# A chunked linear recurrence: its triangular inverses in 32x32 diagonal blocks on 32x32 array tiles, in a new order

## What is computed

```python
def step(S, inp):
    r_t, w_t, k_t, v_t, kk_t, a_t = inp
    sa = jnp.einsum("bhvk,bhk->bhv", S, -kk_t)
    S = (S * w_t[:, :, None, :] + sa[..., None] * (kk_t * a_t)[:, :, None, :]
         + v_t[..., None] * k_t[:, :, None, :])
    o_t = jnp.einsum("bhvk,bhk->bhv", S, r_t)
    return S, o_t
```

## Time and profile before

| | |
|---|---|
| median of three runs | 2034.57 us |
| the profiled execution | 2037.52 us, of which the span is 2035.8 us |
| mean granted TensorE clock | 0.979 |
| PE / PEld busy | 93% / 80% |
| DVE / ACT / POOL busy | 50% / 40% / 12% |
| DMA | 505.55 MB, mean 248 GB/s |
| recurrence, from the span's start | about 526 to 880 us |

### The profile page before, as it was taken

How to read it: one execution, slowest core, us unless ns; L and a number is a source line. 1 busy time by engine, 2 the same in 40 slices (tenths; PEclk the granted TensorE clock), 3 DMA queues, 4 the chain that set the end, 5 groups by cost and what they waited for, 6 DMA issues and landing times.

```text
span 2035.8 us, 49583 instructions
## 1 busy us (share of the span) xinstructions
PE 1890.3 (93%) x20798; PEld 1623.3 (80%) x20798; DVE 1014.0 (50%) x1676; ACT 814.9 (40%) x1436; POOL 244.5 (12%) x308
## 2 busy tenths in 40 slices
PE   7999999999999999999999999999999899777797
PEld 6988999999888888879998676776777677343597
DVE  6644463544455555624544643434445444577344
ACT  4234232334555555523333333333333444555233
POOL 0200000000243444413200000000000000010032
PEclk8999999999999999989999999999999999899899
DMA  7535455544133322105488999999999999999541
GB/s 283 172 135 172 167 172 171 169 162 162 55 100 91 91 88 85 53 22 191 151 328 318 419 419 416 405 425 425 425 424 426 399 420 380 416 366 374 237 145 73
DMA packets 122383, 505.55 MB, mean 248 GB/s; under 512 B 15969, under 2 KB 55266, under 8 KB 76898
## 3 DMA queue, kind: packets, MB, share of 16 engines
q1 hardware_dynamic: 122178, 502.60, 64.6%
HBM read 470.24 MB, written 32.32 MB: 247 GB/s over the span
## 4 chain that ended last, share of the span: by engine, by line
PE 30%; DMA 17%; DVE 2%; issue 2%; SPq 2%; ACT 1%; DVEq 0%; ACTq 0%
DMA at_vraw<-in_cache_v 17%; PE psP L2502 8%; PE psP L2503 7%; PE psP L2504 7%; PE at_psO L2552 5%; PE at_psS L2531 3%; SPq L1915 1%; PE psP L2597 0%; DVE wlo L2264 0%; PE at_psT L2543 0%; DVE at_o_new L2419 0%; SPq L1933 0%; SPq L2000 0%; SPq L1955 0%; ACT whi L2090 0%
## 5 line engine op out<-in xcount | busy, mean ns | idle before, releaser
L2502 PE MATMUL psP<-xhi,whi 128*128 128x320 f32 x1488 | 475.4, 319 | 2.5 <-DVE xlo L2389 1.9
L2504 PE MATMUL psP<-xhi,wlo 128*128 128x320 f32 x1488 | 460.6, 310 | 0.0
L2503 PE MATMUL psP<-xlo,whi 128*128 128x320 f32 x1488 | 460.4, 309 | 0.0
L2502 PEld LDWEIGHTS psP<-xhi,whi 128*128 128x128 f32 x1488 | 280.3, 188 | 65.8 <-issue 65.1
L2264 DVE TENSOR_TENSOR wlo<-wraw,whi 128x2048 fp32r<-128x2048 f32 x92 | 213.0, 2315 | 206.2 <-ACT whi L2090 206.0
L2090 ACT ACTIVATE whi<-wraw 128x2048 fp32r<-128x2048 f32 x92 | 176.0, 1913 | 275.4 <-PE psP L2504 274.1
L2503 PEld LDWEIGHTS psP<-xlo,whi 128*128 128x128 f32 x1488 | 280.6, 189 | 0.1
L2504 PEld LDWEIGHTS psP<-xhi,wlo 128*128 128x128 f32 x1488 | 280.2, 188 | 0.0
L131 PE MATMUL psP<-xhi,whi 128*128 128x320 f32 x704 | 218.1, 310 | 3.0 <-DVE wlo L166 2.3
L132 PE MATMUL psP<-xlo,whi 128*128 128x320 f32 x704 | 217.5, 309 | 0.0
L133 PE MATMUL psP<-xhi,wlo 128*128 128x320 f32 x704 | 217.5, 309 | 0.0
(11 more groups left out here) (359 smaller groups left out, 3255.8 us busy)
## 6 DMA issues: line engine op xcount, KB each, us to landing
wraw<-in_weights SPq DMA_DIRECT2D x160, 1024.0 KB, 6.1
at_kraw<-in_cache_k SPq DMA_DIRECT2D x96, 1024.0 KB, 11.3
at_vraw<-in_cache_v SPq DMA_DIRECT2D x94, 1024.0 KB, 10.8
at_kraw<-in_cache_k SPq DMA_DIRECT2D x64, 512.0 KB, 9.9
at_vraw<-in_cache_v SPq DMA_DIRECT2D x62, 512.0 KB, 10.4
rw_s0t<-in_s0T SPq DMA_DIRECT2D x16, 256.0 KB, 3.1
o_wkv_s<-rw_SN SPq DMA_DIRECT2D x16, 256.0 KB, 2.3
resT<-in_xT SPq DMA_DIRECT2D x4, 640.0 KB, 5.8
```

Of the source, the lines that this page charges most:

```text
L2502: pe.matmul(out, wh, c_.xhi[:, kc, :], start=(kc == 0), stop=False)
L2503: pe.matmul(out, wh, c_.xlo[:, kc, :], start=False, stop=False)
L2504: last = pe.matmul(out, wl, c_.xhi[:, kc, :], start=False, stop=(kc == NM - 1))
```

## The change

1. The inverse is made only for the 32x32 diagonal blocks of A: all of D, Dt, D2, D2t, D4t, W, Y, FI, Yt, E, Et, E2t, Z, XD, XDt are compact, 32 columns a chunk on 128 partitions (four blocks: two for each head). A new product `AA` makes the diagonal blocks of A, masked by VectorE into D (inside blocks of 8) and `F` (the rest).
2. The products D2, W, D4t, Y (five chunks) and E, Z1, E2t, X (four chunks) run by `by_fourths` on 32x32 tiles, four products to a chunk. E2, E4t and Z2 are gone: with four blocks of 8 in 32 tokens, E^4 is zero.
3. The transposed copies Dt, D2t, Yt, Et and X1t come from VectorE's 32x32 transposes, SBUF to SBUF, in place of TensorE products and ScalarE copies.
4. The corner block of X (second half from first half of a head's 64 tokens) is X22 A21 X11, by two products `Ht` and `XB` on 64x64 tiles with A12 (masked on ScalarE) and Ht's right half held at the identity; ScalarE writes X's two halves (`Xa`, `XB`). GpSimd spreads Y of chunk 4 into X (`Y4`).
5. `s4` leaves out the quadrant that D of chunk 4 came from.
6. `ORDER` is written anew for all steps. Masks and two constants more are made on GpSimd.

The diff, cut to its core:

```diff
 ORDER = """
-F.a.sq F.a.ka1 R.t.U0 R.a.Q4 R.a.SA4 R.t.Q4 R.a.O0 P.t.AB R.t.SA0 R.g.Vnx R.v.U0 F.v.cs R.t.U4 P.t.s4 R.t.S0
...
+R.t.U0 R.t.Q4 P.t.AA P.t.AB R.g.Vnx R.a.Q4 F.a.sq R.v.U0 R.t.U4 P.v.D R.t.SA0 F.t.ss P.g.ID R.v.SA0 P.v.Dt R.t.S0
+P.v.F R.v.U4 P.t.D2 R.v.ST0 F.v.ssm R.t.U1 R.t.SA4 R.t.O0 F.a.ln R.v.U1 P.v.FR R.t.SA1 R.a.SA4 P.t.Vn R.a.O0 R.a.SP1
+R.v.SA1 R.g.SAx P.a.D2 R.t.S1 R.t.O4 R.v.ST1 P.v.KK R.t.U2 R.a.O4 R.a.SP2 P.a.Vn R.t.SN P.v.D2t P.a.A12 R.v.U2 F.a.kk0
+F.a.ka1 R.t.SA2 R.v.SNa P.t.W P.t.D4t R.v.SA2 P.v.W R.g.SNb P.a.D4t R.t.S2 P.t.Y R.v.ST2 R.a.SP3 R.t.U3 P.v.Y F.a.rn
+R.t.O2 R.v.U3 P.g.Y4 P.v.Yt R.t.O1 F.g.k2 R.a.O2 R.t.SA3 R.a.O1 P.t.E R.v.SA3 F.v.cs R.t.O3 P.a.E P.t.Kn R.a.O3 F.v.kk
+R.t.mean P.v.Et P.a.Kn F.g.ka F.v.rk F.a.Pi P.t.E2t R.v.cen P.t.Z1 F.g.csm P.a.E2t P.t.s4 R.a.csq P.v.Z1 F.a.Pc P.t.X
+F.g.Kz R.t.var F.a.Pm P.v.X P.v.s3 R.t.S3 F.v.Bz F.g.Rz R.a.lnv P.t.Bn P.v.X1t R.v.ST3 R.a.rstd P.t.Ht F.t.bon R.v.on
+P.a.Ht P.t.XB R.a.ong F.v.bonus P.a.Bn F.v.Az R.g.oy P.a.XB P.a.Xa R.g.y R.a.xh R.v.xl
...
-        D, Dt, D2, D2t, D4t, W = (sb(x, [P, CH, L]) for x in ("D", "Dt", "D2", "D2t", "D4t", "W"))
-        Yt, E, Et = (sb(x, [P, NCH, L]) for x in ("Yt", "E", "Et"))
+        D, Dt, D2, D2t, D4t, W, Y = (sb(x, [P, CH, HL]) for x in ("D", "Dt", "D2", "D2t", "D4t", "W", "Y"))
+        FI, Yt, E, Et, E2t, Z, XD, XDt = (sb(x, [P, NCH, HL]) for x in ("FI", "Yt", "E", "Et", "E2t", "Z", "XD", "XDt"))
+        A12, Ht = sb("A12", [P, NCH, L]), sb("Ht", [P, NCH, L])
...
+                    elif name == "Dt":
+                        Q.v.wait(dve, "D", t)
+                        Q.v.done(dve.transpose(flat(Dt[:]), flat(D[:])), name)
...
+                def by_fourths(out, lhs, rhs, n):
 
                     for c in range(n):
+                        for r in fourths:
+                            last = pe.matmul(out[r, c * HL:c * HL + HL], lhs[r, c], rhs[r, c], start=True, stop=True)
+                    return last
+
+                def corner(out, lhs, rhs):
+
+                    for c in range(NCH):
                         for r in halves:
+                            last = pe.matmul(out[r, c * HL:c * HL + HL], lhs[r, c], rhs[r, c], start=True, stop=True)
                     return last
...
+                    elif name == "AA":
+                        F.v.wait(pe, "Az", t)
+                        F.v.wait(pe, "Bz", t)
+                        for c in range(CH):
+                            for g, rows in enumerate(fourths):
+                                r, cols = halves[g // 2], slice(HL * (g % 2), HL * (g % 2) + HL)
+                                last = pe.matmul(ps[rows, c * HL:c * HL + HL], BZ[j][r, c, cols], ar[r, c, 0, cols],
+                                                 start=True, stop=True)
...
                     elif name == "D2":
-                        Q.a.wait(pe, "Dt", t)
-                        Q.t.done(each(ps, Dt, D, CH), name)
-                    elif name == "D2t":
-                        Q.a.wait(pe, "Dt", t)
-                        Q.t.done(each(ps, D, Dt, CH), name)
+                        Q.v.wait(pe, "Dt", t)
+                        Q.t.done(by_fourths(ps, Dt, D, CH), name)
...
+                    elif name == "Ht":
+                        Q.a.wait(pe, "A12", t)
+                        Q.v.wait(pe, "X1t", t)
+                        Q.t.done(corner(ps, A12, XDt), name)
+                    elif name == "XB":
+                        Q.a.wait(pe, "Ht", t)
+                        Q.v.wait(pe, "X", t)
+                        Q.t.done(corner(ps, Ht, XD), name)
...
                         elif name[0:2] == "SA":
                             if c == 0:
-                                Q.v.wait(pe, "X", t)
+                                Q.a.wait(pe, Q.a.last("Xa", "XB"), t)
```

More of the change, by code:

```diff
@@ L328 @@
 ORDER = """
-F.a.sq F.a.ka1 R.t.U0 R.a.Q4 R.a.SA4 R.t.Q4 R.a.O0 P.t.AB R.t.SA0 R.g.Vnx R.v.U0 F.v.cs R.t.U4 P.t.s4 R.t.S0
[L330 to L337, removed]
+R.t.U0 R.t.Q4 P.t.AA P.t.AB R.g.Vnx R.a.Q4 F.a.sq R.v.U0 R.t.U4 P.v.D R.t.SA0 F.t.ss P.g.ID R.v.SA0 P.v.Dt R.t.S0
[6 more added lines that the diff above has]
+P.a.Ht P.t.XB R.a.ong F.v.bonus P.a.Bn F.v.Az R.g.oy P.a.XB P.a.Xa R.g.y R.a.xh R.v.xl
+""".split()
 AT = {x: k / len(ORDER) for k, x in enumerate(ORDER)}
@@ L396, in products_of_chunk @@
     return pe.matmul(out, wl, c_.xhi[:, kc, :], start=False, stop=(kc == NM - 1))
-READ_BY = {"AB": ("v", "D", "FR", "KK"), "s4": ("v", "D4s", "s3"), "Vn": ("a", "Vn"), "Bn": ("a", "Bn"),
[4 rows of a table removed]
-           "SN": ("v", "SNa"), "mean": ("v", "cen"), "var": ("a", "lnv")}
+READ_BY = {"AB": "v.FR v.KK a.A12", "s4": "v.s3", "AA": "v.D v.F", "Vn": "a.Vn", "Bn": "a.Bn", "Kn": "a.Kn",
+           "D2": "a.D2", "W": "v.W", "D4t": "a.D4t", "Y": "v.Y", "E": "a.E", "Z1": "v.Z1", "E2t": "a.E2t",
+           "X": "v.X", "Ht": "a.Ht", "XB": "a.XB", "Q4": "a.Q4", "U4": "v.U4", "SA4": "a.SA4", "O4": "a.O4",
+           "SN": "v.SNa", "mean": "v.cen", "var": "a.lnv"}
 for _c in range(NCH):
-    READ_BY |= {f"U{_c}": ("v", f"U{_c}"), f"SA{_c}": ("v", f"SA{_c}"), f"S{_c}": ("v", f"ST{_c}"),
-                f"O{_c}": ("a", f"O{_c}")}
+    READ_BY |= {f"U{_c}": f"v.U{_c}", f"SA{_c}": f"v.SA{_c}", f"S{_c}": f"v.ST{_c}", f"O{_c}": f"a.O{_c}"}
 class Banks:
@@ L495, in make_masks @@
     made(pool.tensor_copy(m3[:, 2], m3[:, 0]))
-    made(pool.tensor_copy(mFI[:, 1], mSI[:, 1]))
-    made(pool.tensor_tensor(mFI[:, 0], mSI[:, 0], m8[:], ALU.subtract))
+    made(pool.memset(c_.side[:], 0.0))
+    for g in range(4):
+        rows, cols = slice(HL * g, HL * g + HL), slice(HL * (g % 2), HL * (g % 2) + HL)
+        made(pool.tensor_copy(c_.mD[rows, :], m8[rows, cols]))
+        made(pool.tensor_copy(c_.mF[rows, :], mSI[rows, 0, cols]))
+        made(pool.tensor_copy(c_.I4[rows, :], c_.ident[rows, rows]))
+        made(pool.memset(c_.side[rows, g % 2:g % 2 + 1], 1.0))
+    made(pool.tensor_tensor(c_.mF[:], c_.mF[:], c_.mD[:], ALU.subtract))
     made(pool.memset(keep[:], 1.0))
@@ L1392, in free_p @@
                     if tile >= 0:
-                        eng, *by = READ_BY[x]
-                        for y in by:
-                            (Q.v if eng == "v" else Q.a).wait(pe, y, tile)
+                        for y in READ_BY[x].split():
+                            (Q.v if y[0] == "v" else Q.a).wait(pe, y[2:], tile)
             def free_r(name, t):
@@ L1401, in free_r @@
                     if tile >= 0:
-                        eng, *by = READ_BY[x]
-                        for y in by:
-                            (R.v if eng == "v" else R.a).wait(pe, y, tile)
+                        for y in READ_BY[x].split():
+                            (R.v if y[0] == "v" else R.a).wait(pe, y[2:], tile)
             def over_channels(out, mat, x):
@@ L1508, in products @@
                     elif name == "E2t":
                         Q.a.wait(pe, "E", t)
[L1510 to L1520 removed]
+                        Q.v.wait(pe, "Et", t)
@@ L1521, in products @@
+                        Q.t.done(by_fourths(ps, E, Et, NCH), name)
+                    elif name == "X":
                         Q.a.wait(pe, "E2t", t)
                         Q.v.wait(pe, "Z1", t)
-                        Q.t.done(each(ps, D2t, W, NCH), name)
-                    elif name == "X":
-                        Q.a.wait(pe, "E4t", t)
-                        Q.v.wait(pe, "Z2", t)
-                        Q.t.done(each(ps, D4t, Dt, NCH), name)
+                        Q.t.done(by_fourths(ps, E2t, Z, NCH), name)
+                    elif name == "Ht":
[6 more added lines that the diff above has]
+                        Q.t.done(corner(ps, Ht, XD), name)
```

194 lines of the change are left out of this document (114 added, 80 removed), and 4 rows, old and new, of the table READ_BY.

## The result

The changed kernel is slower: 2111.10 us (median of four runs, 2106.52 to 2116.84) against 2033.41 (four runs), a ratio of 1.0384 [1.0357, 1.041]. The prediction was 1982, faster. The profiled execution spans 2107.1 us at a mean granted clock of 0.954 (before 2035.8 and 0.979). The time is lost in the recurrence, which reaches to about 958 us in place of 880.

The account below looks back on a forecast made before the run. TensorE was taken to bound the recurrence, the U0-to-xl run close beside: 17.1 x 1.12, taken as slots of 19.0 for 22.34 us, saves 50 us plus 2.5 in slot 1; 2037.5 - 52.8 = 1984.7 profiled, median 1982, range 1958 to 2025.

Parts of the forecast that it names:

- E2t: Small-tile TensorE product in a slot, among the 328 records at 8 ns each; shares one tile-size visit with Z1.
- The sum of TensorE's work: TensorE's work in a recurrence slot: 19.98 us before, 17.1 after, with 2.62 for 328 small records, 1.33 for tile-size changes.
- The first rival: Every small record costs 28 to 29 ns whatever its size; TensorE's slot sum 24.0 us, time 2070; 8 in 100.
- The transposes and the narrow VectorE steps: On VectorE in each slot: five transposes 1.51 us, narrowed steps 2.25 where about 3.5 before; VectorE's total 13.3 us.
- the new waits: SA0 waits for XB's copy, about 3 us of cover; D2, E, Z1, Ht wait for transposes queued on VectorE.
- the rate of the 328: TensorE's records on 32x32 and 64x32 tiles in a slot: 8 ns each, 2.62 us together.
- The clock rival: More waits and smaller tiles drop TensorE's clock in every slot, losing 2 to 4 us each; about 2030; 8 in 100.
- The factor of 1.12: Slot length over TensorE's sum, 22.34 against 19.98 us before; kept for the new slot, 17.1 x 1.12 = 19.1 us.
- the run: VectorE's in-order chain from U0 to xl in a slot, the second bound: 16.7 us, or 17 with U0 itself.

Follow-up runs that it names:

- the kernel with the early load: The changed kernel with the load of s0t moved to the head of SyncE's part of a slot; 2067.97 us, ratio 1.0167 against the kernel before.
- the filler: The changed kernel with nine unread 128x128 f32 products added on TensorE ahead of Q4's wait; 2080.00 us, one run.
- the kernel before with the late load: The kernel before with the load of s0t moved behind the wait for y, at the end of SyncE's part of a slot; 2125.58 us, one run.
- half the records: The kernel with the early load, its by_fourths group steps made as half as many records on 64x64 tiles (output not the reference's); 2025.28 us, one run.
- the run's end cut off: The kernel of 2024.03 with xh and xl done one slot later and the order planned anew; 1994.74 us, ratio 0.9809 against the kernel before.
- the kernel of 2024.03: The change's algebra in full squares on 64x64 tiles, s0t loaded early, order planned anew; 2024.03 us, ratio 0.9948 against the kernel before.
- the fourth stretch of the small products: Last of four 320-product stretches put into the kernel before ahead of the recurrence: 64x64 tiles, 32 moving columns; whole kernel 2120.24 us, one run.

## Why the prediction was wrong

**The sum of TensorE's work was nearly right.** A record within a group costs (0.55 - 0.21) / 39 = 8.7 ns where 8 was taken. A group's distance to the next is mostly more than its records: 40 records of W take 0.51 us to the start of D4t, on the same tiles, 0.16 more than 40 x 8.7 ns; E2t's 32 take 0.27 to the start of Z1, nothing more (711.09 and 711.36 in the kernel with the early load). Nine groups are 328 x 8.7 ns = 2.9 us, with at most 9 x 0.17 for their ends 4.4 us, against 2.62 + 1.33 = 3.95 forecast. The first 32x32 record also comes some 0.1 us later behind a group of 64x64 tiles than a 64x64 record does (729.76 to 729.97 against 0.12), so the sum may be a us above the forecast 17.1, and still far under 27.49. The first rival, a price of 25 to 29 ns for each record, fell as such: the Trainium skill ("TensorE: Matmul & The Clock Gate", section "Wait — 56ns, not 53.3ns?") has matmuls start no closer than some 25 ns, and four 32x32 tiles start them 8.3 ns apart. But over a longer stretch the records do come at 27 ns or slower, for another reason, and the rival's warning that their number costs was the right one. It had 8 in 100.

**The transposes and the narrow VectorE steps were right.** By line and shape, kernel after, 560 to 850 us:

```profile
L1347 DVE STREAM_TRANSPOSE rw_Dt<-rw_D 128x160 f32<-128x160 f32 x10 | 3.3, 334 | 0.0
L1359 DVE STREAM_TRANSPOSE rw_XDt<-rw_XD 128x128 f32<-128x128 f32 x11 | 3.3, 302 | 0.0
```

0.33 and 0.30, forecast 0.32 and 0.29. VectorE's busy time is 13.4 us a slot (141.00 x 27.49 / 290), forecast 13.3.

**The step that failed first: the new waits.** The prediction listed what SA0, D2, W, E and Ht would wait for on the engines, and never followed SyncE's queue, though `ORDER` moved `csm`, for which SyncE waits ahead of all its loads. The rows were to be had before: SyncE's waits of the kernel before name `csm` (L1037), and its timeline shows a slot's six loads in this order, `s0t` last, at 719.44. Price: 43.1 us, the fall of the clock included (2111.10 to 2067.97; 39 against the kernel before of each series).

**The step that failed second: a rate without a supply.** "Everything hangs on the rate of the 328" was true of the engine and left out how 8 ns records get to it. The row at which the 8 ns were estimated is a group of 32 behind a pause; it couldn't show the supply, and no rival had it. The 8.6 us that TensorE stood behind packets in the kernel before were a sign. Price: 42.7 us (2067.97 to 2025.28, one run; 45 against the kernel before of each series), some of it clock again, 0.96 against 1.00.

**The clock rival** had the right form ("if the clock fell in every slot for a few us") and nearly the right size for one slot, 2 to 4 us; the filler recovered 1.8. But it was priced as if the waits themselves were free and it came alone, about 2030. It was the waits that dropped the clock, Q4's 2.45 us above all, and a stop of 1.40 us in the kernel with the early load; smaller tiles were not needed for it: the kernel before with the late load has 0.89, and with half the records and no late load it is 1.00.

**The factor of 1.12** doesn't carry over. It is what TensorE's collisions cost while TensorE binds. With 17.4 us of work the slot was 21.4 in place of 19.5, and with the run's end cut off it fell to 20.17. The prediction put the run at 16.7 us "if nobody is in its way"; in the kernel of 2024.03 the slot that it set was 21.4. Two bounds of almost equal length, met by one in-order queue, gave more than the larger of the two here. With the run's end cut off, 20.17 / 17.4 = 1.16.

Without the late load and with half the records the time is 2025.3, and 43 us still separate that from the forecast 1982. No run takes them apart in this kernel. In the one on 64x64 tiles 29.3 of a similar gap (2024.03 to 1994.74) came back when the run was cut and the order planned again; that the changed kernel's rest is the same is likely and not shown.

## What to carry over

When an order is planned anew, follow every queue that waits for its steps, the one that only issues loads too: its last load is as late as its first wait. Count a stream of small instructions twice, by what the engine takes for one and by how fast instructions arrive: in this kernel the groups of 8 ns records lost 42.7 us against half as many records of 26 ns (2067.97 and 2025.28). And before trusting a new bound, look for the second one within 15% of it and for the engine on which both queue.

## What the runs showed of the hardware

- TensorE's instructions arrive in packets of 16 KB, 256 instructions, 1.0 us each (57 packets for 7096 matmul records and 7094 weight loads in 290 us of the changed kernel); TensorE goes on 1.2 to 1.7 us after a packet's end when it has run out. In a long stretch of short records one portion comes every 3.46 us or more, 27 ns for a weight load with its matmul. After a stretch of slower work 241 records came without a gap.
- Records of 32 columns on 64x64 tiles cost (0.72 - 0.22) / 19 = 26 ns, those of 64 columns 29: half the columns bring 3 ns there. On four 32x32 tiles 64 columns cost (1.99 - 0.21) / 127 = 14.0 ns, as in the earlier trace rows, 32 columns 8.3.
- In the fourth stretch of the small products the granted clock was at 0.50 while TensorE was busy all the time (so it ran at 52 ns a record, and not between the first two as expected), behind a stretch in which it had stood half the time. Busy times, columns as in the earlier trace rows:

```profile
520.00:530.00 10.00, 10.00 (x352) 10.00 (x347) 0.00 (x0) 0.00 (x0) 0.00 (x0) 1.00 0.02 5
549.00:560.00 11.00, 11.00 (x233) 10.91 (x232) 0.00 (x0) 0.00 (x0) 0.00 (x0) 0.56 0.01 3
570.00:580.00 10.00, 10.00 (x192) 10.00 (x192) 0.00 (x0) 0.00 (x0) 0.00 (x0) 0.50 0.01 2
```

The first row is the second stretch, 64 columns at 29 ns a record and the full clock; the other two are the fourth, 32 columns at 52 ns. Why the clock didn't come back there isn't known from these runs.
